# Differential attention: the norm sums of split squares as float32r products, ScalarE's weight split placed behind the copies of the probabilities, first weight tiles subtracted by GpSimd

## The chip, the cores and the metric

One NeuronCore of a Trainium2 chip runs the whole program as one launch. The metric is the device time of one execution in microseconds (us), less is better. A change is timed by the median of several executions.

Engines: PE is TensorE, ACT is ScalarE, DVE is VectorE, POOL is GpSimd, SP issues the transfers from memory.

## What is computed

The reference is two transformer blocks of two layers each, over 256 tokens (272 with 16 meta tokens in the second block) of width 1024. The change lies in one mixer of the second block, the differential attention with 8 heads:

```
q, k, v = split(h @ w_in)
q = rms_norm(q.reshape(.., 8, 2, 64), g0);  k = rms_norm(k.reshape(.., 8, 2, 64), g1)
logits = q . k * 64**-0.5 + bias            # two maps m for every head
p = softmax(where(visible, logits, -1e30))
pd = p[0] - lam * p[1]
o = pd @ v                                  # 128 values of a head
o = rms_norm(o, subln) * (1 - lambda_init)
```

Two sums of squares across partitions belong to it: one over the 64 rows of each map for q and k, one over the 128 rows of a head's output.

## The kernel before

The program is written by hand, engine by engine: each engine has one list of instructions, and semaphores say what each waits for. Nothing is reordered: a wait holds up everything behind it on its engine.

**Weights.** All products are made in three float32r products (`product`, L1592 to L1603): high part of the weights by high and low part of the moving side, then low part of the weights by the high part. Weights come in chunks into two slots in turn. For each chunk SP loads `raw` (L381), ACT copies it to `w_hi` (L703), and DVE or POOL subtracts `raw - w_hi` into `w_lo`. SP loads the next chunk of a slot when the low parts of the one before are there (`rest_ready`), ACT overwrites `w_hi` when PE has used it (`weights_used`).

**The mixer (`diff_mixer`, stage "diff").** Chunk i holds the q, k and v columns of head i, three tiles of 128x1024, and PE makes parts 0, 1 and 2 of them in round i. Beside the parts of head i each round does steps of the two heads before: sums of squares, logits and turned values of head h = i-1, turned probabilities, outputs and output sums of head b = i-2. PE's order in a round is: part 0, `sums`(h), part 1, `turn_probs`(b), half of part 2, `logits`(h), `turn_values`(h), `outputs`(b), the rest of part 2, `out_sums`(b). A last stretch behind round 7 finishes heads 6 and 7 between early products of the output projection (`early`).

- `sums` (L1800) multiplies the squares `asq` by `halves`, a 0/1 matrix, in float32: two products of 128x272. `out_sums` (L1844) multiplies `osq` by `ones`, one such product.
- ACT in round i: logarithm and exponential for the norms of h (L855, L856), `y_hi` (L849), copies of the turned probabilities of b (L861, L862), square of the outputs (L872), copies of the values (L877, L878), squares of head i (L881), exponentials of the logits of h (L886), logarithm and exponential for the output norm (L890, L891), and last the weight split of chunk i+2 (L893, the copy itself L703), 128x3072 in one instruction.
- DVE subtracts the first tile of chunks 2 to 7 (`first_tile_of`, L1140), POOL the second and third (L641, L643, the instruction itself L512). Part 0 waits for the first tile (`tile_rest`), part 1 for all three (`rest_ready`, L1753).

```
mm(to, lhsT=w_hi[slot][:, w], rhs=hi[:, k, cols], start=start and i == 0, stop=False)
mm(to, lhsT=w_hi[slot][:, w], rhs=lo[:, k, cols], start=False, stop=False)
ins = mm(to, lhsT=w_lo[slot][:, w], rhs=hi[:, k, cols], start=False, stop=stop and i == len(order) - 1)
```

## Time and profile before

| what | us |
|---|---|
| time, median of 3 runs (lowest, highest) | 1695.86 (1695.57, 1695.9) |
| time of the profiled execution | 1696.9 |
| span of the profiled execution | 1695.1 |
| PE busy | 1671.7 (99%) |
| ACT busy | 835.7 (49%) |
| DVE busy | 953.3 (56%) |
| POOL busy | 736.3 (43%) |

The span runs from the first to the last instruction of the core; the time of the same execution is 1.8 us more. The mixer takes the stretch from about 824 us to 950 us of the span. Records of matmuls overlap: a record of 0.29 us stands every 0.126 us, so what a product takes is read from the distance of the starts.

### The profile page before, as it was taken

How to read it: one execution, taken by the hardware profiler on the slowest of the kernel's cores; microseconds unless marked ns; L12 is line 12 of the kernel's file. 1: busy time of each engine (PE TensorE's matmuls, PEld its weight loads, DVE VectorE, ACT ScalarE, POOL GpSimd, SP SyncE). 2: the span in 40 equal slices, each digit the busy share in tenths (PEclk: the TensorE clock that was granted, in tenths of full speed). 3: DMA queues.
4: the chain of work that ended last, by engine and by line, in shares of the span. 5: the costliest groups of instructions: out<-in, count | busy, mean ns of one | idle time of the engine just before them, and what ended most of it. 6: DMA issues, size and time to landing. Idle time of an engine off the chain costs nothing.

```text
span 1695.1 us, 34373 instructions
## 1 busy us (share of the span) xinstructions
PE 1671.7 (99%) x13441; PEld 1630.9 (96%) x13441; DVE 953.3 (56%) x1188; ACT 835.7 (49%) x1161; POOL 736.3 (43%) x488
## 2 busy tenths in 40 slices
PE   7999999999999999999999999999999999999999
PEld 6999999999999999999999899999999988899999
DVE  6685556633655556545456755455555567665553
ACT  5445454555544544444476644444444446654442
POOL 6235553254555545553332355533554324245520
PEclk9999999999999999999999999999999999999999
DMA  7658876643787756676643466765667741357673
GB/s 205 175 163 231 232 201 187 171 113 100 214 229 195 206 155 174 173 198 174 166 120 89 121 178 173 198 174 149 173 173 195 184 106 51 100 151 196 175 213 110
DMA packets 538562, 283.55 MB, mean 167 GB/s; under 512 B 12112, under 2 KB 532817, under 8 KB 538481
## 3 DMA queue, kind: packets, MB, share of 16 engines
q1 hardware_dynamic: 538065, 281.30, 60.8%
q0 software_dynamic: 352, 1.09, 0.3%
q8 instruction: 59, 0.97, 0.2%
q14 instruction: 22, 0.18, 0.0%
q10 hardware_dynamic: 64, 0.02, 0.0%
HBM read 281.29 MB, written 5.53 MB: 169 GB/s over the span
## 4 chain that ended last, share of the span: by engine, by line
PE 87%; DVE 5%; ACT 4%; DMA 2%; POOL 1%; issue 1%; SPq 0%; POOLq 0%; ACTq 0%; DVEq 0%
PE bank L1600 26%; PE bank L1602 26%; PE bank L1601 25%; DVE w_lo L1113 2%; PE bank L1641 2%; PE bank L1985 2%; ACT w_hi L703 1%; DMA raw<-in_w_down 1%; PE bank L1948 1%; DVE xg_lo L1124 1%; DMA raw<-in_ffn_wi 1%; POOL up L588 1%; PE bank L2018 1%; PE bank L1820 0%; ACT w_hi L1032 0%
## 5 line engine op out<-in xcount | busy, mean ns | idle before, releaser
L1600 PE MATMUL bank<-xg_hi,w_hi 128*128 128x272 f32 (+1 forms) x2520 | 724.2, 287 | 0.2 <-DVE w_lo L1113 0.2
L1602 PE MATMUL bank<-xg_hi,w_lo 128*128 128x272 f32 (+1 forms) x2520 | 718.9, 285 | 0.0
L1601 PE MATMUL bank<-xg_lo,w_hi 128*128 128x272 f32 (+1 forms) x2520 | 717.1, 285 | 0.0
L1113 DVE TENSOR_TENSOR w_lo<-raw,w_hi 128x2048 fp32r<-128x2048 f32 (+3 forms) x200 | 501.2, 2506 | 263.3 <-ACT w_hi L703 263.1
L703 ACT ACTIVATE w_hi<-raw 128x2048 fp32r<-128x2048 f32 (+3 forms) x212 | 442.0, 2085 | 266.7 <-PE bank L1602 262.0
L1600 PEld LDWEIGHTS bank<-xg_hi,w_hi 128*128 128x128 f32 x2520 | 475.2, 189 | 3.0 <-issue 1.5
L1602 PEld LDWEIGHTS bank<-xg_hi,w_lo 128*128 128x128 f32 x2520 | 475.5, 189 | 0.0
L1601 PEld LDWEIGHTS bank<-xg_lo,w_hi 128*128 128x128 f32 x2520 | 474.2, 188 | 0.7
L588 POOL TENSOR_TENSOR up<-gate,up 128x256 f32<-128x256 f32 (+1 forms) x132 | 304.4, 2306 | 253.0 <-ACT gate L1039 252.9
L1600 PE MATMUL bank<-act_hi,w_hi 128*128 128x256 f32 (+1 forms) x1056 | 300.9, 285 | 0.5 <-DVE w_lo L1113 0.2
L1601 PE MATMUL bank<-act_lo,w_hi 128*128 128x256 f32 (+1 forms) x1056 | 300.7, 285 | 0.0
L1602 PE MATMUL bank<-act_hi,w_lo 128*128 128x256 f32 (+1 forms) x1056 | 300.5, 285 | 0.0
L540 POOL TENSOR_TENSOR ssq<-ssq,sq 128x256 f32<-128x256 f32 (+1 forms) x64 | 142.0, 2218 | 241.9 <-ACT sq L718 227.6
L1041 ACT ACTIVATE act_hi<-up 128x256 f32 (+3 forms) x132 | 56.1, 425 | 340.7 <-POOL up L588 340.7
L1600 PEld LDWEIGHTS bank<-act_hi,w_hi 128*128 128x128 f32 x1056 | 198.8, 188 | 1.1 <-DVE w_lo L1113 1.1
L1602 PEld LDWEIGHTS bank<-act_hi,w_lo 128*128 128x128 f32 x1056 | 198.9, 188 | 0.0
L1601 PEld LDWEIGHTS bank<-act_lo,w_hi 128*128 128x128 f32 x1056 | 198.7, 188 | 0.0
L1515 DVE TENSOR_TENSOR gate<-bank,rstd 128x256 f32<-128x256 f32 (+1 forms) x132 | 57.2, 433 | 197.0 <-PE bank L1602 193.3
L512 POOL TENSOR_TENSOR w_lo<-raw,w_hi 128x1024 fp32r<-128x1024 f32 (+3 forms) x27 | 82.1, 3041 | 154.8 <-ACT w_hi L703 128.6
L590 POOL TENSOR_TENSOR act_lo<-up,act_hi 128x256 f32 (+1 forms) x132 | 100.1, 758 | 97.4 <-ACT act_hi L1041 97.4
L1454 DVE SCALAR_TENSOR_TENSOR x<-bank,x 128x256 f32<-128x256 f32 (+3 forms) x80 | 32.9, 427 | 85.9 <-PE bank L1602 85.3
L1124 DVE SCALAR_TENSOR_TENSOR xg_lo<-x,gains,xg_hi (+2 forms) x72 | 64.1, 911 | 7.6 <-ACT xg_hi L723 5.1
(307 smaller groups left out, 1909.1 us busy)
## 6 DMA issues: line engine op xcount, KB each, us to landing
raw<-in_ffn_wi SPq DMA_DIRECT2D x176, 512.0 KB, 4.9
raw<-in_ffn_wo SPq DMA_DIRECT2D x32, 1408.0 KB, 7.1
raw<-in_w_gate SPq DMA_DIRECT2D x44, 512.0 KB, 4.0
raw<-in_w_up SPq DMA_DIRECT2D x44, 512.0 KB, 5.2
raw<-in_w_down SPq DMA_DIRECT2D x16, 1408.0 KB, 7.1
raw<-in_a_w_in SPq DMA_DIRECT2D x24, 512.0 KB, 5.3
raw<-in_a_in SPq DMA_DIRECT2D x20, 512.0 KB, 6.4
raw<-in_w_o SPq DMA_DIRECT2D x16, 512.0 KB, 4.8
```

The source lines that it names most:

```text
L512: return gp.tensor_tensor(w_lo[slot][:, t], raw[slot][:, t], w_hi[slot][:, t].bitcast(F32), ALU.subtract)
L540: gp.tensor_tensor(ssq[:, c], ssq[:, c], sq[:, s, c] if squares is None else squares, ALU.add).then_inc(ssq_ready, 1)
L588: gp.tensor_tensor(up, gate, up, ALU.mult).then_inc(act_full, 1)
L590: gp.tensor_tensor(tile(f.lo, c, f.act_cols), up, tile(f.hi, c, f.act_cols).bitcast(F32), ALU.subtract).then_inc(act_ready, 1)
L703: act.activation(w_hi[slot][:, 0:stage.size], raw[slot][:, 0:stage.size], ACT.Copy).then_inc(head_ready, 1)
L1041: act.activation(tile(f.hi, c, f.act_cols), f.up[:, s, f.act_cols], ACT.Copy).then_inc(act_hi_ready, 1)
L1113: v.tensor_tensor(w_lo[slot][:, 0:n], raw[slot][:, 0:n], w_hi[slot][:, 0:n].bitcast(F32), ALU.subtract).then_inc(rest_ready, 1)
L1124: ins = v.scalar_tensor_tensor(out=tile(lo, d, cols), in0=src, scalar=column(gains, gain + d), in1=tile(hi, d, cols).bitcast(F32), op0=ALU ...
L1515: v.tensor_tensor(f.gate[:, s, f.act_cols], bank[:, 2 * s, 0:n], rstd[:, f.cols], ALU.mult).then_inc(gate_ready, 1)
L1600: mm(to, lhsT=w_hi[slot][:, w], rhs=hi[:, k, cols], start=start and i == 0, stop=False)
L1601: mm(to, lhsT=w_hi[slot][:, w], rhs=lo[:, k, cols], start=False, stop=False)
L1602: ins = mm(to, lhsT=w_lo[slot][:, w], rhs=hi[:, k, cols], start=False, stop=stop and i == len(order) - 1)
```

## The change

The squares are split like the weights: ACT copies `asq` to `asq_hi` and `osq` to `osq_hi` (float32r), POOL subtracts the rest into `asq_lo` and `osq_lo` (`low_squares`, `low_outputs`), and PE adds two float32r products for each old float32 one. This holds for all eight heads of `sums` and for the output sums of heads 0 to 5; those of heads 6 and 7 stay as they were. `out_sums` of head b moves from the end of round b+2 to behind part 0 of round b+3. ACT's weight split of chunks 2 to 7 moves from the end of round i to behind the copies of the turned probabilities of round i+1, and becomes two instructions, the first tile with a signal of its own (`diff_head`). The first tiles of chunks 2 to 7 are subtracted by POOL, no longer by DVE. Two constant matrices are copied to float32r at the start.

```diff
--- before.py
+++ after.py
...
@@ -523,6 +527,8 @@
                                     pattern=[[-1, P]], channel_multiplier=1))
             settle(gp.memset(halves[0:HD, 0:HD], 1.0))
             settle(gp.memset(halves[HD:P, HD:P], 1.0))
+            gp.tensor_copy(halves_r[:, :], halves[:, :])
+            gp.tensor_copy(ones_r[:, :], ones[:, :])
             settle(gp.memset(vis[0:HD, META + HD:KEYS_A], NEG))
             settle(gp.memset(vis[0:HD, KEYS_A + TOK - HD:LOGB], NEG))
             gp.sem_inc(consts, 1)
@@ -635,12 +641,33 @@
             gp.wait_ge(weights_used, st["diff"].first)
             gp.memset(apt0[:, :], 0.0)
             gp.memset(avn[:, 0, :], 0.0).then_inc(a_padded, 1)
+            def low_squares(i):
+                gp.wait_ge(a_sq_hi, i + 1)
+                if i:
+                    gp.wait_ge(a_sums, i)
+                gp.tensor_tensor(asq_lo[:, :, :], asq[:, :, :], asq_hi[:, :, :].bitcast(F32), ALU.subtract).then_inc(a_sq, 1)
+            def low_outputs(b):
+                gp.wait_ge(a_osq_hi, b + 1)
+                if b:
+                    gp.wait_ge(a_osum, b)
+                gp.tensor_tensor(osq_lo[:, :], osq[:, :], osq_hi[:, :].bitcast(F32), ALU.subtract).then_inc(a_osq, 1)
+            low_squares(0)
             for c in range(2, 8):
                 g, n = st["diff"].first + c, KT * P
                 gp.wait_ge(rest_ready, g)
+                gp.wait_ge(diff_head, c - 1)
+                gp.tensor_tensor(w_lo[g % 2][:, 0:n], raw[g % 2][:, 0:n], w_hi[g % 2][:, 0:n].bitcast(F32), ALU.subtract).then_inc(tile_rest, 1)
                 split(g, n, 2 * n)
-                gp.wait_ge(tile_rest, first_tiles(st["diff"], c))
                 split(g, 2 * n, 3 * n).then_inc(rest_ready, 1)
+                if c >= 3:
+                    low_outputs(c - 3)
+                low_squares(c - 1)
+            low_outputs(5)
+            low_squares(7)
             g = st["wo2"].first + 1
             gp.wait_ge(tile_head, 5)
             gp.tensor_tensor(w_lo[g % 2][:, 0:n], raw[g % 2][:, 0:n], w_hi[g % 2][:, 0:n].bitcast(F32), ALU.subtract).then_inc(wo2_tile, 1)
@@ -860,6 +887,12 @@
                         act.wait_ge(a_turned, b + 1)
                         act.activation(apt[:, :], bank[:, 3, 0:384], ACT.Copy)
                         act.activation(apt0[0:META, :], bank[0:META, 4, 0:TOK], ACT.Copy).then_inc(a_pt, 1)
+                    if 1 <= i < 7:
+                        g, n = first + i + 1, KT * P
+                        act.wait_ge(landed[g % 2], chunks.landed[g])
+                        act.wait_ge(weights_used, g - 1)
+                        for t, signal in ((slice(0, n), diff_head), (slice(n, 3 * n), head_ready)):
+                            act.activation(w_hi[g % 2][:, t], raw[g % 2][:, t], ACT.Copy).then_inc(signal, 1)
                     if i == 8:
                         g, n = first + 9, KT * P
                         act.wait_ge(landed[g % 2], chunks.landed[g])
@@ -869,7 +902,14 @@
                             act.activation(w_hi[g % 2][:, t], raw[g % 2][:, t], ACT.Copy).then_inc(signal, 1)
                     if b >= 0:
                         act.wait_ge(a_o, b + 1)
-                        act.activation(osq[:, :], bank[:, 5, 0:TOK], ACT.Square).then_inc(a_osq, 1)
+                        if b:
+                            act.wait_ge(a_osq, b)
+                        squares = act.activation(osq[:, :], bank[:, 5, 0:TOK], ACT.Square)
+                        if b < 6:
+                            settle(squares)
+                            act.activation(osq_hi[:, :], osq[:, :], ACT.Copy).then_inc(a_osq_hi, 1)
+                        else:
+                            squares.then_inc(a_osq, 1)
                     if 0 <= h < 8:
                         act.wait_ge(a_vt, h + 1)
                         if not h:
@@ -878,7 +918,10 @@
                         act.activation(avn[:, 1:3, :], bank[:, 4, P:3 * P].rearrange("p (a b) -> p a b", b=P), ACT.Copy).then_inc(a_v, 1)
                     if i < 8:
                         act.wait_ge(parts_read, 2 * mixer_order(st["diff"], i) + 2)
-                        act.activation(asq[:, :, :], aqkv[:, i % 2, 0:2, :], ACT.Square).then_inc(a_sq, 1)
+                        if i:
+                            act.wait_ge(a_sq, i)
+                        settle(act.activation(asq[:, :, :], aqkv[:, i % 2, 0:2, :], ACT.Square))
+                        act.activation(asq_hi[:, :, :], asq[:, :, :], ACT.Copy).then_inc(a_sq_hi, 1)
                     if 0 <= h < 8:
                         act.wait_ge(a_max, h + 1)
                         for t, c in enumerate((COL_A, COL_B, COL_M)):
@@ -889,7 +932,7 @@
                         act.wait_ge(a_osum, b + 1)
                         settle(act.activation(oln[:, :], bank[:, 3, 0:TOK], ACT.Ln, bias=eps[:, 0:1], scale=1.0 / P))
                         act.activation(oln[:, :], oln[:, :], ACT.Exp, scale=-0.5).then_inc(a_orms, 1)
-                    if i < 7:
+                    if i == 6:
                         split_ahead(first + i)
                     if i == 8:
                         tile_ahead(st["wo2"])
@@ -1321,9 +1364,7 @@
                         rest_of_output(b - 1)
                     take_part(0)
                     if 0 <= h < 8:
-                        if h < 6:
-                            first_tile_of(stage.first + h + 2)
-                        elif h == 6:
+                        if h == 6:
                             v.wait_ge(rest_ready, stage.first + h + 2)
                             split_ahead(stage.first + h)
                         v.wait_ge(a_logits, h + 1)
@@ -1802,7 +1843,8 @@
                     if h:
                         pe.wait_ge(a_max, h)
                     for m in range(2):
-                        ins = mm(bank[:, 6 + m, 0:TOK], lhsT=halves[:, :], rhs=asq[:, m, :], start=True, stop=True)
+                        mm(bank[:, 6 + m, 0:TOK], lhsT=halves_r[:, :], rhs=asq_hi[:, m, :], start=True, stop=False)
+                        ins = mm(bank[:, 6 + m, 0:TOK], lhsT=halves_r[:, :], rhs=asq_lo[:, m, :], start=False, stop=True)
                     ins.then_inc(a_sums, 1)
                 def turn_values():
@@ -1843,7 +1885,11 @@
                 def out_sums():
                     pe.wait_ge(a_osq, h + 1)
-                    mm(bank[:, 3, 0:TOK], lhsT=ones[:, :], rhs=osq[:, :], start=True, stop=True).then_inc(a_osum, 1)
+                    if h >= 6:
+                        mm(bank[:, 3, 0:TOK], lhsT=ones[:, :], rhs=osq[:, :], start=True, stop=True).then_inc(a_osum, 1)
+                        return
+                    mm(bank[:, 3, 0:TOK], lhsT=ones_r[:, :], rhs=osq_hi[:, :], start=True, stop=False)
+                    mm(bank[:, 3, 0:TOK], lhsT=ones_r[:, :], rhs=osq_lo[:, :], start=False, stop=True).then_inc(a_osum, 1)
                 return sums, turn_values, logits, turn_probs, outputs, out_sums
@@ -1858,15 +1904,17 @@
                     sums, turn_values, logits, _, _, _ = steps[i - 1] if i else [None] * 6
-                    _, _, _, turn_probs, outputs, out_sums = steps[i - 2] if i > 1 else [None] * 6
-                    for step in (lambda: part(0), sums, lambda: part(1), turn_probs,
-                                 lambda: part(2, range(4)), logits, turn_values, outputs, lambda: part(2, range(4, KT)), out_sums):
+                    _, _, _, turn_probs, outputs, _ = steps[i - 2] if i > 1 else [None] * 6
+                    out_sums = steps[i - 3][5] if i > 2 else None
+                    for step in (lambda: part(0), out_sums, sums, lambda: part(1), turn_probs,
+                                 lambda: part(2, range(4)), logits, turn_values, outputs, lambda: part(2, range(4, KT))):
                         if step:
                             step()
                 sums, turn_values, logits, turn_probs, outputs, out_sums = steps[7]
                 early(2, 0, range(5))
+                steps[5][5]()
                 sums()
                 early(2, 1, range(5))
                 steps[6][3]()
```

The order of the instructions on POOL before, for chunks 2, 3 and the start of 4 (slots 0 and 1 in turn; L512 is the subtraction of one tile):

```order
L512 TENSOR_TENSOR w_lo0<-raw0,w_hi0 128x1024 [waits head_ready,rest_ready]
L512 TENSOR_TENSOR w_lo0<-raw0,w_hi0 128x1024 [waits head_ready,tile_rest]
L512 TENSOR_TENSOR w_lo1<-raw1,w_hi1 128x1024 [waits head_ready,rest_ready]
L512 TENSOR_TENSOR w_lo1<-raw1,w_hi1 128x1024 [waits head_ready,tile_rest]
L512 TENSOR_TENSOR w_lo0<-raw0,w_hi0 128x1024 [waits head_ready,rest_ready]
```

In the changed kernel POOL has these for chunks 3 and 4; L663 and L516 are the tiles of the weights, L656 the outputs' low part, L649 the squares':

```order
L663 TENSOR_TENSOR w_lo1<-raw1,w_hi1 128x1024 [waits diff_head,rest_ready]
L516 TENSOR_TENSOR w_lo1<-raw1,w_hi1 128x1024 [waits head_ready] x2
L656 TENSOR_TENSOR osq_lo<-osq,osq_hi 128x272 [waits a_osq_hi]
L649 TENSOR_TENSOR asq_lo<-asq,asq_hi 128x544 [waits a_sums,a_sq_hi]
L663 TENSOR_TENSOR w_lo0<-raw0,w_hi0 128x1024 [waits diff_head,rest_ready]
L516 TENSOR_TENSOR w_lo0<-raw0,w_hi0 128x1024 [waits head_ready] x2
L656 TENSOR_TENSOR osq_lo<-osq,osq_hi 128x272 [waits a_osum,a_osq_hi]
L649 TENSOR_TENSOR asq_lo<-asq,asq_hi 128x544 [waits a_sums,a_sq_hi]
```

Two instructions of a chunk have become five, and the low parts of the squares, for which PE waits behind part 0, stand behind the three tiles of the next chunk.

On PE, the end of part 0, the sums and the start of part 1, before:

```order
L1600 MATMUL bank<-xg_hi,w_hi 128x272
L1601 MATMUL bank<-xg_lo,w_hi 128x272
L1602 MATMUL bank<-xg_hi,w_lo 128x272
L1805 MATMUL bank<-asq,halves 128x272 [waits a_max,a_sq]
L1805 MATMUL bank<-asq,halves 128x272
L1600 MATMUL bank<-xg_hi,w_hi 128x272 [waits parts_read,rest_ready]
```

And in the changed kernel:

```order
L1642 MATMUL bank<-xg_lo,w_hi 128x272
L1643 MATMUL bank<-xg_hi,w_lo 128x272
L1891 MATMUL bank<-osq_hi,ones_r 128x272 [waits a_osq]
L1892 MATMUL bank<-osq_lo,ones_r 128x272
L1846 MATMUL bank<-asq_hi,halves_r 128x272 [waits a_max,a_sq]
L1847 MATMUL bank<-asq_lo,halves_r 128x272
L1846 MATMUL bank<-asq_hi,halves_r 128x272
L1847 MATMUL bank<-asq_lo,halves_r 128x272
L1641 MATMUL bank<-xg_hi,w_hi 128x272 [waits parts_read,rest_ready]
```

Both sums now stand in one place, the output sums ahead; `a_osq` and `a_sq` are signals of POOL's two subtractions there.

On ACT, the copies of the turned probabilities and what follows, in the changed kernel (before, L872's square followed the copies at once, and the split of 128x3072 stood behind the logarithm and exponential of `oln`):

```order
L888 ACTIVATE apt<-bank 128x384 [waits a_turned]
L889 ACTIVATE apt<-bank 16x272
L895 ACTIVATE w_hi<-raw 128x1024 [waits weights_used,landed1]
L895 ACTIVATE w_hi<-raw 128x2048
L907 ACTIVATE osq<-bank 128x272 [waits a_osq,a_o]
L910 ACTIVATE osq_hi<-osq 128x272 [waits a_step]
L917 ACTIVATE avn<-bank 16x128 [waits a_vt]
```

The weight copy now waits, through its place, for the turned probabilities.

## Rows read from the trace of the kernel before

**Rows 1.** Windows: us, busy of PE, PEld, DVE, ACT, POOL, granted clock, DMA.

```profile
872.60:886.30 13.70, 13.70 (x107) 12.91 (x105) 8.46 (x20) 9.53 (x26) 4.76 (x2) 1.00 0.44 116
```

**Rows 2.** Waits of PE from 827 to 950 us: total, times, longest.

```profile
PE bank L1820 <- DVE aqkv L1317: 0.6, 1, 0.6
PE bank L1641 <- DVE apd L1347: 0.5, 1, 0.5
```

**Rows 3.** Timeline of PE: start, us, line, tile, count.

```profile
836.65 1.08 PE L1805 MATMUL bank<-asq,halves 128*128 128x272 f32 x4
...
879.56 0.92 PE L1641 MATMUL bank<-ident,apd 128*128 128x128 f32 x6
...
885.91 0.62 PE L1846 MATMUL bank<-osq,ones 128*128 128x272 f32 x2
...
886.49 0.28 PE L1601 MATMUL bank<-xg_lo,w_hi 128*128 128x272 f32 x1
...
889.39 1.08 PE L1805 MATMUL bank<-asq,halves 128*128 128x272 f32 x4
...
890.43 0.29 PE L1601 MATMUL bank<-xg_lo,w_hi 128*128 128x272 f32 x1
...
916.91 1.08 PE L1805 MATMUL bank<-asq,halves 128*128 128x272 f32 x4
```

**Rows 4.** Timeline of ACT in one round, idle before in brackets.

```profile
875.75 2.76 ACT L703 ACTIVATE w_hi<-raw 128x3072 fp32r<-128x3072 f32 x1
878.41 0.66 ACT L855 ACTIVATE bank<-bank,eps 128x544 f32<-128x544 f32 x1
879.10 0.61 ACT L856 ACTIVATE bank<-bank 128x544 f32<-128x544 f32 x1
...
880.51 0.49 ACT L861 ACTIVATE apt<-bank 128x384 f32<-128x384 f32 x1 [0.47 <-PE bank L1641]
880.90 0.37 ACT L862 ACTIVATE apt<-bank 16x272 f32<-16x272 f32 x1
884.60 0.40 ACT L872 ACTIVATE osq<-bank 128x272 f32<-128x272 f32 x1 [3.32 <-PE bank L1842]
```

**Rows 5.** Timeline of POOL in the same round, and two rows of the last mixer.

```profile
878.64 2.39 POOL L512 TENSOR_TENSOR w_lo<-raw,w_hi 128x1024 fp32r<-128x1024 f32 x1 [7.15 <-ACT w_hi L703]
882.89 2.37 POOL L512 TENSOR_TENSOR w_lo<-raw,w_hi 128x1024 fp32r<-128x1024 f32 x1 [1.86 <-DVE w_lo L1140]
...
1420.39 1.29 POOL L659 TENSOR_TENSOR qs<-qs 128x512 f32<-128x512 f32 x1 [5.22 <-ACT qs L966]
1421.64 2.13 POOL L668 TENSOR_TENSOR bias<-bias,score 128x288 f32<-128x288 f32 x2
```

**Rows 6.** Groups by line and form: count, busy us, mean ns.

```profile
L588 POOL TENSOR_TENSOR up<-gate,up 128x272 f32<-128x272 f32 x66 | 153.6, 2328 | 136.1 <-ACT gate L1039 136.1
L590 POOL TENSOR_TENSOR act_lo<-up,act_hi 128x272 f32 x66 | 51.2, 776 | 49.2 <-ACT act_hi L1041 49.2
L512 POOL TENSOR_TENSOR w_lo<-raw,w_hi 128x1024 fp32r<-128x1024 f32 x18 | 42.8, 2379 | 75.2 <-ACT w_hi L703 60.8 <-DVE w_lo L1140 11.0 <-ACT w_hi L800 3.4
L869 ACT ACTIVATE w_hi<-raw 128x1024 fp32r<-128x1024 f32 x2 | 2.0, 1039 | 0.0
```

**Rows 7.** Source line L881: min, median, max ns, first and last start.

```profile
L881 ACT ACTIVATE asq<-aqkv x8: 657/657/658, 832.4 to 927.0; 128x544 f32<-128x544 f32 x8
```

**Rows 8.** Timeline: one subtraction of DVE beside POOL and alone.

```profile
864.88 2.38 POOL L512 TENSOR_TENSOR w_lo<-raw,w_hi 128x1024 fp32r<-128x1024 f32 x1 [7.10 <-ACT w_hi L703]
...
866.80 0.76 DVE L1305 TENSOR_TENSOR y_lo<-oy,y_hi 128x272 fp32r<-128x272 f32 x1
...
921.00 0.43 DVE L1305 TENSOR_TENSOR y_lo<-oy,y_hi 128x272 fp32r<-128x272 f32 x1
```

**Rows 9.** Groups of DVE by form, 800 to 950 us: scaling and combining the probabilities.

```profile
L1344 DVE TENSOR_SCALAR apd<-al,ars 128x272 f32<-128x272 f32 x8 | 2.8, 356 | 0.0
L1347 DVE SCALAR_TENSOR_TENSOR apd<-al,ars,apd 128x272 f32<-128x272 f32 x8 | 4.0, 496 | 0.0
```

More of the change, by code:

```diff
@@ L127, in two_blocks @@
         ident, ones, halves, tri = (sb(n, [P, P]) for n in ("ident", "ones", "halves", "tri"))
+        halves_r, ones_r = sb("halves_r", [P, P], F32R), sb("ones_r", [P, P], F32R)
         eps, gains, small = sb("eps", [P, 1]), sb("gains", [P, P + KT]), sb("small", [P, 4])
@@ L162, in two_blocks @@
             aqkv = sb("aqkv", [P, 2, 3, TOK], F32, ph)
+            asq_hi, asq_lo = (sb(n, [P, 2, TOK], F32R, ph) for n in ("asq_hi", "asq_lo"))
+            osq_hi, osq_lo = (sb(n, [P, TOK], F32R, ph) for n in ("osq_hi", "osq_lo"))
             asq, avn = sb("asq", [P, 2, TOK], F32, ph), sb("avn", [P, 3, P], F32, ph)
```

1 line of the change is left out of this document (added).

## The prediction

> **What bounds the kernel now.** I read the windows first. In one round of the mixer [rows 1] PE is busy in all of 13.70 us at full granted clock, while POOL works 4.76 us of it, ACT 9.53 and DVE 8.46. The waits of PE [rows 2] say the same over the whole mixer: 1.1 us in two places, both behind the last round. So PE's own work sets the time here, and every microsecond that goes from PE counts, as long as nothing else becomes slower than a round. The round's length comes from the starts of the `sums` in the timeline of PE [rows 3]: two rounds lie between 889.39 and 916.91, 13.76 us each. The timelines of ACT and POOL [rows 4, 5] show who has room. ACT makes the weight copy of 2.76 us as the last thing of a round, which holds up the logarithm behind it, and stands idle for 3.32 us between the copies of the probabilities and the squares of the outputs. POOL waits 7.15 us for the copy, does a tile, waits 1.86 us for DVE's tile, and does another.
>
> **What PE saves.** The two float32 products of `sums` start at 889.39; the second product behind them starts at 890.43, and a float32r product stands every 0.126 us (24 of part 0 fit between 886.36 and 889.39, where 886.36 is 886.49 less 0.126). So they take 890.43 - 0.13 - 889.39 = 0.91 us. The output sum takes 886.36 - 885.91 = 0.45 us [rows 3]. Four float32r products take 0.50 and two take 0.25. That is 0.41 us for each of 8 heads and 0.20 for each of 6: **4.5 us** in all. PE's own round becomes 13.15 us.
>
> **What POOL gets.** Before, two tiles of 2.38 us [rows 5, 6]. Now three, the low part of the outputs and the low part of the squares. A subtraction of the first one's size took 0.78 (128x272) and a tile of 1024 columns 2.38, both in rows 6; along this line 544 columns take 1.36. A round of POOL is 7.14 + 0.78 + 1.36 = 9.3 us, which fits in 13.15. But its place decides, not its sum. By the order of the instructions, the low squares that `sums`(h) waits for stand on POOL behind all three tiles of the next chunk, and those wait for a weight copy that stands on ACT behind the turned probabilities, which PE makes behind part 1, behind the `sums` before. That closes a loop from one `sums` to the next:
>
> - `sums` 0.50, part 1 3.03 (24 products);
> - turned probabilities, to ACT's first copy: 880.51 - 879.56 = 0.95 [rows 3, 4];
> - both copies, to the weight copy: 0.39 (880.90 - 880.51), and 0.27 (0.37 less the 0.10 by which ACT's records overlap);
> - weight copy of the first tile 1.04 [rows 6], to POOL 0.13 (878.51 to 878.64) [rows 4, 5];
> - three tiles 7.14, low outputs 0.78, low squares 1.36, less 0.16 for four overlaps of POOL's records (1421.64 begins 0.04 before the end of the one of 1420.39) [rows 5];
> - to PE 0.03.
>
> The sum is **15.46 us**, against 13.76 before: 1.70 us more. PE's work in it is 13.15, so PE stands for 2.3 us in each such round, first for the low outputs (`out_sums` is ahead of `sums` on PE), then for the low squares; everything behind it on PE is queued, part 1 first. The saving of PE is swallowed whole in these rounds. The loop turns five times (chunks 3 to 7, between `sums`(1) and `sums`(6)): **+8.5 us**.
>
> **Before the loop.** `sums`(0) keeps its place at 836.65: the squares start at 832.4 [rows 7], the high copy (a copy of the same shape; I take the square's 0.66) ends by 833.8, the low part by 835.3. Chunk 2 waits for no probabilities: from 836.65 the sums' records end 0.67 later, logarithm and exponential take 0.66 and 0.61 with gaps of 0.03 [rows 4], weight copy 1.04, three tiles and low squares 8.5, hand-overs 0.16, overlaps -0.2: PE can start `sums`(1) at about 848.3. It started at 916.91 - 5 x 13.76 = 848.1. **+0.2 us**.
>
> **Behind the loop.** PE saves 0.41 for each of `sums`(6) and (7) and 0.20 for the output sum of head 5. Against that `sums`(7) waits for the square, its copy (0.66) and POOL (1.36); PE arrives after 15 early products (1.9 us), and I lay this out to a wait of 0.5. The exponentials of head 6 stand on ACT behind two more copies (0.40 as the square of L872, and 0.66), and this stretch is where PE already waited for DVE [rows 2]: between 0 and 1.1 us, I take 0.8, for PE arrives earlier too. **+0.3 us**, bounds -1.0 and +0.8.
>
> **What costs nothing.** ACT has 1.06 us more to copy in each round and hides it in the idle 3.32 us and in PE's new waits. The weight copy in two pieces begins 5.4 us later than before (881.17 against 875.75), and the raw slot is free later by about as much, with a whole round of cover before ACT wants the next load. If that cover went, the copy's start would slip and with it the loop, one for one. DVE loses six tiles, which nobody waits for. The two copies at the start of the program are short and POOL idles there.
>
> **The sum.** 0.2 + 8.5 + 0.3 = +9.0 us. The sum is made on the profiled execution, whose time is 1696.9 (span 1695.1); the median of the runs is 1695.86, 1.0 less, and I take the difference to be the same there: **1704.9 us**.
>
> **Unknown prices.** POOL's subtraction of 544 columns is not in the mixer's trace: not below 0.78, the price of half of it; above, there is a row where 272 columns take 2.33 us (L588) [rows 6], in the feed-forwards, beside DVE's long subtractions of weights. I take 1.36, since two of POOL's forms lie on one line and DVE has no long subtraction left in these rounds. Each 0.1 us is 0.5 us of time.
>
> **Where DVE and POOL meet.** DVE's `y_lo` takes 0.43 alone and 0.76 when POOL's tile runs: it starts at 866.80, the tile ends at 867.26, and 867.26 + 0.3 is its end [rows 8]. So they exclude each other. In the new round the three instructions that combine the probabilities on DVE (0.50 at the most [rows 9]) come due while POOL is at the low squares. By my layout POOL is there first, and DVE waits up to 1 us, covered by part 1. Were DVE first, POOL would wait 0.5 in each of five rounds. The sum counts nothing for it.
>
> The Trainium skill, "GPSIMD Engine Reference", section "Key points", says that the two share their SBUF interfaces, and that VectorE's instructions in a 2-port performance mode contend as well as those with two inputs in SBUF. The second half agrees with `y_lo`; for the first half no row here has POOL beside such an instruction.
>
> **Rivals.**
>
> *DVE delays POOL.* The scaling of the probabilities has one input, takes 0.36 where the combining takes 0.50 for the same size [rows 9], and starts about half a microsecond after the exponentials, just when POOL goes from the low outputs to the low squares. If it excludes POOL too, POOL waits 0.36 in each of five rounds: +1.8, 1706.7. With one combining instead, +2.5: 1707.4. All six in a row would be up to 2.6 a round and 1718, which needs POOL to lose each time. The page's rule named above would make the scaling one of these. Chance 0.26.
>
> *The gain lands.* If POOL's chain fitted in PE's round, the time would be 1695.86 - 4.5 + 0.9 for the stretch behind: 1692.3, faster. The place is POOL's five instructions of 9.1 us; it decides at 15.46 - 13.15 = 2.3 us less, or 0.46 off each of the five. For it: the sum of POOL's work is far from a round. Against: 18 tiles have a mean of 2.379 and nothing of the chain overlaps. Chance 0.04.
>
> *It cancels.* A loop of 13.8 us, 1.7 less than mine, gives about 1696.4. That would need POOL's small subtractions and the hand-overs to be almost free. Chance 0.03.
>
> *POOL's subtractions are slow.* At 2.33 for each of the two (the L588 row), the loop is 2.5 us longer: +12.6, 1717.5. Against: DVE has no long instruction there. Chance 0.04.
>
> **Numbers.** My forecast has the rest, 0.63. Its own bounds are the loop within 0.3 us a round (five times) and the stretch behind: 1702.4 to 1707.2. To leave out no more than 2 in 10 with the first rival in, and allowing for collisions of more than one instruction, the range is 1702.0 to 1710.0. A measurement of this kernel can tell some 0.2% from no change, 3.4 us. Faster: 0.04. Same: 0.03. Slower: 0.93.
>
> **What would show it.** The distance of the `sums` on PE is about 15.4 us between the second and the seventh. PE waits for POOL's low outputs for about 1.2 us and then for the low squares for about 1.1 us, five times each. POOL runs its five instructions of a chunk without a gap and idles some 6.3 us before the first, for ACT's weight copy. The four products of `sums` take 0.50. ACT's copy follows the probabilities without idle time. The forecast is wrong if the distance is 13.2 to 13.8, if PE waits for part 1's weights instead, or if the low squares take other than 1.3 to 1.6 us.

## The result and the profile after

The changed kernel takes **1710.8 us** (median of 4 runs, 1710.24 to 1713.82) against 1695.88 for the kernel before (4 runs beside them, 1695.57 to 1696.38): ratio 1.009, 95% interval 1.0078 to 1.0102. It is slower, as forecast, but by 14.9 us and not by 9.0, and 0.8 us above the top of the range. The profiled execution took 1710.96 us with a span of 1709.2, 14.1 more than that of before.

The whole loss lies in the mixer. The first update of `x` behind it, on DVE, stands at 950.14 before and at 964.48 after:

```profile
950.14 0.79 DVE L1454 SCALAR_TENSOR_TENSOR x<-bank,x 128x272 f32<-128x272 f32 x2 [1.17 <-PE bank L1602]
```

```profile
964.48 0.79 DVE L1495 SCALAR_TENSOR_TENSOR x<-bank,x 128x272 f32<-128x272 f32 x2 [1.17 <-PE bank L1643]
```

Both kernels start the first `sums` at 836.65, so the mixer's stretch from there became 127.83 us instead of 113.49: 14.34 more. The timeline of PE after the change, at the first product of each head's `sums` (start, us, line, tile, and in brackets the idle time before it), shows where:

```profile
836.65 0.29 PE L1846 MATMUL bank<-asq_hi,halves_r 128*128 128x272 f32 x1
...
848.41 0.39 PE L1846 MATMUL bank<-asq_hi,halves_r 128*128 128x272 f32 x1 [0.56 <-POOL asq_lo L649]
...
863.98 0.40 PE L1846 MATMUL bank<-asq_hi,halves_r 128*128 128x272 f32 x1 [0.79 <-POOL asq_lo L649]
...
879.57 0.40 PE L1846 MATMUL bank<-asq_hi,halves_r 128*128 128x272 f32 x1 [0.78 <-POOL asq_lo L649]
...
893.86 0.39 PE L1891 MATMUL bank<-osq_hi,ones_r 128*128 128x272 f32 x1 [1.12 <-POOL osq_lo L656]
...
895.15 0.39 PE L1846 MATMUL bank<-asq_hi,halves_r 128*128 128x272 f32 x1 [0.77 <-POOL asq_lo L649]
...
912.22 0.39 PE L1846 MATMUL bank<-asq_hi,halves_r 128*128 128x272 f32 x1 [0.78 <-POOL asq_lo L649]
...
929.32 0.40 PE L1846 MATMUL bank<-asq_hi,halves_r 128*128 128x272 f32 x1 [0.79 <-POOL asq_lo L649]
```

The starts of the heads' `sums` are 15.57, 15.59 and 15.58 us apart, then 17.07 and 17.10; before, 13.76 each [rows 3]. The waits of PE from 824 to 970 us (total, times, longest) have two new entries in place of next to nothing [rows 2]:

```profile
PE bank L1891 <- POOL osq_lo L656: 5.6, 5, 1.1
PE bank L1846 <- POOL asq_lo L649: 4.8, 7, 0.8
```

POOL and ACT in the round before 895.15 are the forecast loop: the copies of the probabilities, the weight copy straight behind them, then five instructions of POOL without a gap. ACT first:

```profile
884.15 0.49 ACT L888 ACTIVATE apt<-bank 128x384 f32<-128x384 f32 x1 [1.94 <-PE bank L1682]
884.54 0.37 ACT L889 ACTIVATE apt<-bank 16x272 f32<-16x272 f32 x1
884.82 2.84 ACT L895 ACTIVATE w_hi<-raw 128x1024 fp32r<-128x1024 f32 x2
```

and POOL, whose idle time before the first tile is the 6.48 in brackets:

```profile
886.00 2.38 POOL L663 TENSOR_TENSOR w_lo<-raw,w_hi 128x1024 fp32r<-128x1024 f32 x1 [6.48 <-ACT w_hi L895]
888.33 4.76 POOL L516 TENSOR_TENSOR w_lo<-raw,w_hi 128x1024 fp32r<-128x1024 f32 x2
893.04 0.76 POOL L656 TENSOR_TENSOR osq_lo<-osq,osq_hi 128x272 fp32r<-128x272 f32 x1
893.76 1.33 POOL L649 TENSOR_TENSOR asq_lo<-asq,asq_hi 128x544 fp32r<-128x544 f32 x1
```

What I had not foreseen stands in the windows by round (us, busy of PE, PEld, DVE, ACT and POOL with counts, granted clock, DMA share, GB/s). Up to 895 us the clock is 1.00, as in [rows 1]. Then it is 0.90, 0.89 and 0.89:

```profile
863.90:879.50 15.60, 13.68 (x105) 12.65 (x105) 8.25 (x20) 11.01 (x28) 9.11 (x6) 1.00 0.40 105
879.50:895.00 15.50, 13.69 (x105) 12.65 (x105) 8.15 (x20) 10.92 (x28) 9.02 (x6) 1.00 0.38 98
895.00:912.00 17.00, 15.18 (x105) 14.16 (x105) 8.14 (x20) 10.93 (x27) 9.01 (x6) 0.90 0.36 94
912.00:928.00 16.00, 14.69 (x103) 13.88 (x103) 7.15 (x19) 10.51 (x26) 7.99 (x6) 0.89 0.21 59
928.00:943.00 15.00, 14.20 (x98) 13.30 (x98) 9.81 (x18) 8.43 (x19) 2.93 (x3) 0.89 0.50 140
...
896.00:900.00 4.00, 4.00 (x22) 4.00 (x21) 2.92 (x9) 1.67 (x3) 0.00 (x0) 0.57 1.12 279
```

The last row shows for the first of these rounds that it is one piece of some 3.4 us at the lower level of 1.2 GHz. It begins half a microsecond after the sums, in part 1 of the round. In the timeline of PE the products stand 0.126 us apart ahead of it and 0.227 in it:

```profile
896.12 0.29 PE L1641 MATMUL bank<-xg_hi,w_hi 128*128 128x272 f32 x1
896.25 0.39 PE L1642 MATMUL bank<-xg_lo,w_hi 128*128 128x272 f32 x1
896.44 0.43 PE L1643 MATMUL bank<-xg_hi,w_lo 128*128 128x272 f32 x1
896.66 0.43 PE L1641 MATMUL bank<-xg_hi,w_hi 128*128 128x272 f32 x1
...
899.61 0.33 PE L1642 MATMUL bank<-xg_lo,w_hi 128*128 128x272 f32 x1
```

15 products took 899.61 - 896.25 = 3.36 us and would have taken 1.89: **1.5 us** a time, three times. So the 14.34 us are: 0.32 up to `sums`(1) (848.41 against 848.09), five rounds at 15.58 - 13.77 = 1.81, 9.05 in all, three stretches at the low clock, 4.5 (two of them in these rounds, the third behind `sums`(6)), and 0.4 more behind `sums`(6).

### The profile page after: what moved, and what is told of

Its sections match the earlier page's. It is cut to its first block, busy times and chain, and to the rows that moved or that the text cites. A ratio compares the mean times of both kernels' runs of the same rounds, so it can differ in the third digit from the quotient of the medians.

```text
span 1709.2 us, 34429 instructions
## 1 busy us (share of the span) xinstructions
PE 1673.7 (98%) x13441; PEld 1633.0 (96%) x13441; DVE 950.9 (56%) x1182; ACT 844.6 (49%) x1181; POOL 765.7 (45%) x510
## 4 chain that ended last, share of the span: by engine, by line
PE 84%; DVE 5%; ACT 4%; POOL 3%; DMA 2%; issue 1%; SPq 0%; POOLq 0%; ACTq 0%; DVEq 0%
PE bank L1641 25%; PE bank L1643 25%; PE bank L1642 25%; DVE w_lo L1156 2%; PE bank L2033 2%; PE bank L1682 2%; ACT w_hi L730 1%; POOL w_lo L516 1%; DMA raw<-in_ffn_wi 1%; DVE xg_lo L1167 1%; POOL up L594 1%; POOL w_lo L663 1%; PE bank L2066 1%; ACT w_hi L1075 0%; DMA xin<-in_x 0%
## 5 line engine op out<-in xcount | busy, mean ns | idle before, releaser
L730 ACT ACTIVATE w_hi<-raw 128x2048 fp32r<-128x2048 f32 (+3 forms) x206 | 425.5, 2065 | 266.8 <-PE bank L1643 261.2
L516 POOL TENSOR_TENSOR w_lo<-raw,w_hi 128x1024 fp32r<-128x1024 f32 (+3 forms) x27 | 82.0, 3049 | 96.3 <-ACT w_hi L730 81.0
```

Of the source, the lines that this page charges most:

```text
L516: return gp.tensor_tensor(w_lo[slot][:, t], raw[slot][:, t], w_hi[slot][:, t].bitcast(F32), ALU.subtract)
L730: act.activation(w_hi[slot][:, 0:stage.size], raw[slot][:, 0:stage.size], ACT.Copy).then_inc(head_ready, 1)
```

## The experiments

Each edit is made on the changed kernel. "Mixer" is the stretch from the first `sums` to the first update of `x` behind it: 113.49 us before, 127.83 after. It is read from one profiled execution of each kernel. The medians take in the rest of the program too, where low stretches of the clock come and go: the window from 0 to 20 us has 0.83 before and after, 0.91 with the waits filled and 1.00 with DVE's tile.

### The idle time of PE filled with dummy products

```diff
+                    def fill(n, start):
+                        if i >= start:
+                            pe.wait_ge(a_max, i - 1)
+                            for _ in range(n):
+                                mm(bank[:, 6, 0:TOK], lhsT=ones_r[:, :], rhs=xg_hi[:, 0, :], start=True, stop=True)
-                    for step in (lambda: part(0), out_sums, sums, ...
+                    for step in (lambda: part(0), lambda: fill(8, 3), out_sums, lambda: fill(6, 3), sums, ...
```

> The change with PE kept at work where it waits: in rounds 3 to 7 PE makes 8 products of 128x272 into a bank that nobody reads before the output sums, and 6 before the norm sums (about 1.0 and 0.75 us, no more than the two waits). Idle theory: the clock dips of the changed kernel come from PE standing idle for 1.1 and 0.8 us in every round. Then the distance of the norm sums is 15.6 us in all rounds, the granted clock is 1.00 throughout the mixer, and the time is 1710.8 - 4.6 = 1706.2. Rival, the dips have another cause than PE's idle time: the distances of 17.1 us and the granted clock of 0.89 to 0.90 stay, 1710.8.

Measured: 1705.43 us (before: 1696.85), ratio 1.0052, interval 1.0035 to 1.0069: 5.4 us below the change, of which the mixer has 4.3 (123.50 us). The `sums` stand 15.6 us apart in every round (893.85, 909.46, 925.08), and the windows that had the low clock now read

```profile
895.00:911.00 16.00, 15.82 (x124) 14.79 (x124) 8.65 (x22) 11.37 (x29) 9.12 (x5) 1.00 0.41 108
911.00:927.00 16.00, 15.82 (x124) 14.80 (x124) 8.64 (x21) 12.02 (x28) 9.13 (x5) 1.00 0.25 70
```

The 14 dummy products a round stand where PE waited for POOL anyhow, and the low clock is gone. The clock's share is shown, and it comes from PE's waits: the rest of the kernel is the same. What is left is +8.6 us by the medians and +10.0 in the mixer, around the forecast of +9.0. The two differ because the profiled execution of this kernel reaches the mixer 1.43 us earlier than that of before (835.22 against 836.65), with a shorter low stretch at its start.

### The products in float32 again, the rest of the change kept

The high copies on ACT and the low parts on POOL go; the three tiles on POOL, the two-piece weight copy behind the probabilities and the later place of the output sum stay.

```diff
-                        mm(bank[:, 6 + m, 0:TOK], lhsT=halves_r[:, :], rhs=asq_hi[:, m, :], start=True, stop=False)
-                        ins = mm(bank[:, 6 + m, 0:TOK], lhsT=halves_r[:, :], rhs=asq_lo[:, m, :], start=False, stop=True)
+                        ins = mm(bank[:, 6 + m, 0:TOK], lhsT=halves[:, :], rhs=asq[:, m, :], start=True, stop=True)
```

> The change with the products of the squares in float32 again (no high copies on ACT, no low parts on POOL); the moved weight copy, the third tile on POOL and the moved output sums stay. Queue theory: what costs is that PE waits for the low parts behind three tiles. Then PE waits for nothing on POOL, the distance of the norm sums is PE's 13.76 us and the time 1696.0, within 1 of before. Rival, the weights themselves come too late (three tiles on POOL behind the late copy): PE waits before part 1 in each round, 1698 or more.

Measured: 1696.65 us, ratio 1.0002, interval 0.9992 to 1.0012. PE waits for POOL nowhere, and the `sums` in its timeline start at 861.60, 875.36 and 889.13, 13.76 and 13.77 apart.

The mixer takes 113.97 us, 0.5 more than before. So the moved tiles and the moved copy cost next to nothing by themselves. They cost when the low parts that PE needs are queued behind them.

### ScalarE's weight copy ahead of the wait for the turned probabilities

```diff
-                    if b >= 0:
-                        act.wait_ge(a_turned, b + 1)
...
                     if 1 <= i < 7:
                         g, n = first + i + 1, KT * P
...
+                    if b >= 0:
+                        act.wait_ge(a_turned, b + 1)
```

> The change with ACT's weight copy moved ahead of the wait for the turned probabilities (it stands right behind the exponential of the norms). Queue theory: the loop loses part 1, the turned probabilities and their copies, so that POOL's chain fits in a round; PE waits at most 0.5 us for the low squares in a round, distance 13.2 to 13.7 us, no clock dips, time about 1695.6 (within 1.5). Rival, DVE and POOL shut each other out so often that the chain stays longer than 14.5 us: 1702 or more.

Measured: 1696.97 us, ratio 1.0004, interval 0.9995 to 1.0014; mixer 113.9. The distances are 13.26 to 14.00 us, up to 0.3 more than expected, and the longest wait 0.8, not 0.5. One block of ACT moved by one place turns +14.9 us into +0.1: the turned probabilities no longer close the loop. The waits of PE for POOL shrink from 10.4 us to

```profile
PE bank L1846 <- POOL asq_lo L649: 2.0, 4, 0.8
```

### The low parts between POOL's second and third tile

```diff
                 split(g, n, 2 * n)
-                split(g, 2 * n, 3 * n).then_inc(rest_ready, 1)
                 if c >= 3:
                     low_outputs(c - 3)
                 low_squares(c - 1)
+                split(g, 2 * n, 3 * n).then_inc(rest_ready, 1)
```

> The change with POOL's low outputs and low squares placed between the second and the third tile of a chunk. The sums then don't wait; part 1 waits for the third tile instead. Queue theory: the loop loses the hand-over to the sums and 0.5 us of sums, distance about 15.0 us, one wait of about 1.8 us before part 1 in place of two of 1.1 and 0.8; 1695.9 + 8 = 1704 without clock dips. Idle theory of the clock: PE idles as much in a round as in the change, in one piece, so dips come too, up to +4.6: 1704 to 1708.6. If low parts behind the tiles were not what PE waits for, the distance would stay 15.6.

Measured: 1705.67 us, ratio 1.0053, interval 1.0036 to 1.007; distance 15.08 (896.00, 911.07, 926.15), one stretch at the low clock. It lies in the first round of the loop (16.60 us, from 849.24), and the five waits of the same length behind it bring none. The wait changes its name and stays:

```profile
PE bank L1641 <- POOL w_lo L516: 9.3, 6, 1.6
```

The same 9.1 us of POOL end in the round, and what comes last is now the third tile. Another order of POOL's own five instructions doesn't open the loop.

### The first tile back on DVE

```diff
-                gp.wait_ge(diff_head, c - 1)
-                gp.tensor_tensor(w_lo[g % 2][:, 0:n], ...).then_inc(tile_rest, 1)
...
+                            v.wait_ge(diff_head, h + 1)
+                            v.tensor_tensor(w_lo[g % 2][:, t], ...).then_inc(tile_rest, 1)
```

> The change with the first tile of chunks 2 to 7 subtracted by DVE again (as soon as its high part is there), POOL keeps the second and third. Queue theory: the loop loses a tile of 2.33 us but now begins with the second piece of ACT's copy (1.9 us, less 0.1), because POOL has nothing to do before it: distance about 15.0 us, PE waits about 1.1 and 0.7, time 1702.0 without clock dips. If it was the number of tiles on POOL alone that mattered, the distance would be 13.2 and the time 1693. Idle theory of the clock: idle time is only 0.5 us a round less than in the change, so one to three dips of 1.5 us: 1703.5 to 1706.5.

Measured: 1703.79 us, ratio 1.0044, interval 1.0028 to 1.0059; distance 15.03, clock 1.00 in the whole mixer, mixer 120.6. POOL has 6.75 us to do in 16 and PE still waits for it:

```profile
PE bank L1849 <- POOL asq_lo L649: 4.8, 7, 0.8
PE bank L1894 <- POOL osq_lo L656: 2.9, 5, 0.6
```

A tile less on POOL gives 0.55 us a round, not 2.38, since the two that are left wait for the second piece of ACT's copy, 1.8 us behind the first (POOL idles 8.28 us, not 6.48). The share of busy time misleads here: the place of the work decides.

### Dummy products only ahead of the output sum

> The change with PE kept at work for about 1.0 us before the output sums in rounds 3 to 7, but left idle for 0.8 us before the norm sums. The distance by the queue stays 15.6. Idle theory: the less PE stands idle, the fewer dips; with 0.8 us in one piece a round fewer than three: 1706 to 1708. Rival, the dips come from the wait before the norm sums alone, or from a change of work between waits: still three, 1710.8.

Measured: 1706.99 us (1706.62 to 1709.23), ratio 1.0061, interval 1.0045 to 1.0076. PE is idle for 0.8 us five times, right ahead of the norm sums, which the waits show without a releaser:

```profile
PE bank L1846 <- issue: 4.1, 5, 0.8
```

and the granted clock is 1.00 in each window from 848 to 928 us. So the second wait, alone and of this length, brought no low clock in this trace. The mixer takes 123.43 us, the same as with both waits filled, so the 1.6 us by which the median is above that kernel's lie outside it. One low stretch there is at 1500 to 1520 us (0.91), in another mixer; the filled kernel has one too, at 1400 to 1420, so this alone does not explain them.

### More work at the end of POOL's round

An extra subtraction of the squares' size, the same one twice, ahead of the low outputs.

```diff
+                gp.wait_ge(a_sq_hi, c)
+                gp.wait_ge(a_sums, c - 1)
+                settle(gp.tensor_tensor(asq_lo[:, :, :], asq[:, :, :], asq_hi[:, :, :].bitcast(F32), ALU.subtract))
                 if c >= 3:
                     low_outputs(c - 3)
```

> The change with POOL's low squares done twice for chunks 2 to 7, the extra one ahead of the low outputs (1.33 us and about 0.1 to settle). Queue theory: the loop is that much longer, distance 17.0 us, +1.4 in each of six rounds, 1710.8 + 8.5 = 1719.3 with three clock dips as in the change. Idle theory of the clock: with 3.3 us idle a round there are more dips, up to one in every round, each 1.5 us: 1719 to 1724. Rival, POOL's queue isn't what sets the rounds: less than +4.

Measured: 1725.05 us (1723.55 to 1725.62), ratio 1.0165, interval 1.0149 to 1.018. The first round of the loop has 16.99 us (849.53 to 866.52), the slope of one subtraction as expected. The next has 19.53, since from here on the clock is low in every round:

```profile
863.60:879.00 15.40, 13.12 (x81) 12.20 (x82) 9.00 (x18) 7.29 (x14) 6.29 (x5) 0.78 0.40 103
879.00:895.00 16.00, 12.71 (x90) 11.80 (x89) 7.22 (x15) 9.06 (x24) 7.99 (x6) 0.89 0.37 99
```

The time is 1 us above the range that I expected. Low stretches cost more than the 1.5 us that I had put in for each: against the 16.99 us of the first round, the four next have 2.54, 1.45, 2.34 and 1.34 more, and in windows of 1 us the stretches last some 6.8 and 3.4 us in turn. Over the traces so far more idle time of PE in a round goes with more low stretches in the mixer: none in the filled kernels (0 and 0.8 us idle) and with DVE's tile (1.35), one with the low parts in the middle (1.6), three in the change (1.9), and here (3.0 to 3.3) one at each of the five pairs of waits. These are counts in one execution each, and no threshold is read from them.

### A first attempt at a version below both

Early copy, DVE's tile, and head 7's squares in float32, together.

> What the queue theory says should beat both: the split squares, with ACT's weight copy right behind the exponential of the norms (as in the early copy run), the first tile on DVE, and the squares of head 7 in float32 as before. POOL's chain fits in PE's round: no wait of PE from the second round on over 0.3 us, distance 13.2 to 13.4 us, no dips, 1.7 us below before: 1694.3. If the early copy holds up the copies of the probabilities by more than the 0.2 us that I lay out, or DVE and POOL shut each other out, it comes out at before's time or above.

Measured: 1696.07 us (11 runs), ratio 0.9996, interval 0.9987 to 1.0005. The distance is 13.5, but it is no faster than before by anything that was measured: 1.1 us went to four waits of PE for the copies of the probabilities, now behind the weight copy on ACT, and about 1.5 to one low stretch, behind the last round (0.90 and 0.89 from 927 to 943 us), where PE waits for DVE first.

### The copy back at the end of the round

```diff
-                    if 1 <= i < 7:
-                        g, n = first + i + 1, KT * P
...
+                    elif i < 6:
+                        g, n = first + i + 2, KT * P
                         for t, signal in ((slice(0, n), diff_head), (slice(n, 3 * n), head_ready)):
```

> The change with ScalarE's weight copy (still in its two pieces) put back to the end of a round, behind the logarithm and exponential of the output norm, as before; products, low parts and the three tiles on POOL stay. Loop theory (the chain sums, part 1, turned probabilities, weight copy, three tiles, low parts binds): the copy no longer waits for the turned probabilities, POOL starts its tiles several us earlier in each round, POOL's work of 9.1 us fits in a round, and the distance of the sums falls from 15.58 to PE's own 13.2 to 13.4. PE waits for POOL at most 0.2 us a round, the clock stays at 1.00 in rounds 3 to 7. Time: before minus 2.0 us (five rounds at about -0.4 us) plus 1.0 (head 7's squares and the stretch behind) = 1694.9 against a before of 1695.9, range 1693.5 to 1697. Rival (the amount of work given to POOL, not its place, makes the loss): distance stays at 15 or more, time above 1702. Second rival (PE waits of 0.5 us or more remain at the low squares, as with the early copy): distance 13.6 and 1696 to 1697.

Measured: 1707.21 us (before: 1697.72), ratio 1.006, interval 1.0047 to 1.0074. **A clear miss**, and by neither of the rivals: the time is that of the first one (above 1702), but its distance of 15 or more is not there. PE hardly waits for POOL any more, it waits for the turned probabilities:

```profile
PE bank L1682 <- DVE apd L1388: 10.6, 7, 5.6
PE bank L1846 <- POOL asq_lo L649: 1.8, 2, 1.2
```

DVE's timeline has the reason, in the first such round and in a later one. Three combinings, which took 0.93 us before and after, take 7.11 and 3.08:

```profile
848.33 0.71 DVE L1385 TENSOR_SCALAR apd<-al,ars 128x144 f32<-128x144 f32 x3
849.07 7.11 DVE L1388 SCALAR_TENSOR_TENSOR apd<-al,ars,apd 128x144 f32<-128x144 f32 x3
...
868.56 0.71 DVE L1385 TENSOR_SCALAR apd<-al,ars 128x144 f32<-128x144 f32 x3
869.31 3.08 DVE L1388 SCALAR_TENSOR_TENSOR apd<-al,ars,apd 128x144 f32<-128x144 f32 x3
```

and POOL's timeline shows what ran meanwhile:

```profile
848.90 2.39 POOL L663 TENSOR_TENSOR w_lo<-raw,w_hi 128x1024 fp32r<-128x1024 f32 x1 [2.06 <-ACT w_hi L936]
851.24 4.91 POOL L516 TENSOR_TENSOR w_lo<-raw,w_hi 128x1024 fp32r<-128x1024 f32 x2
...
869.97 2.38 POOL L663 TENSOR_TENSOR w_lo<-raw,w_hi 128x1024 fp32r<-128x1024 f32 x1 [2.88 <-ACT w_hi L936]
872.31 4.91 POOL L516 TENSOR_TENSOR w_lo<-raw,w_hi 128x1024 fp32r<-128x1024 f32 x2
```

The combinings end when POOL's tile ends (872.35 and 872.39), in the first round when all three do (856.15 and 856.18). In narrower windows of that round each of the three combinings stands for one tile of POOL: they start at 849.07, 851.38 and 853.88 and take 2.39, 2.57 and 2.30 us. It is the meeting that [rows 8] show for `y_lo`, but `y_lo` is wanted late and the probabilities at once. The two-piece copy had let POOL begin 1.8 us before the whole copy was made, just in the way. The first gap is 20.83 us (846.89 to 867.72), with 5.55 idle and a granted clock of 0.79 in the window behind it; the four after it are 14.4. Together, 7.06 + 4 x 0.64 = 9.6 us. What this adds to the change: its move of the copy behind the probabilities keeps POOL's tiles clear of the combinings, and pays for it with the loop.

### The same with head 7's squares in float32

> The kernel of the run before, with the squares of head 7 alone summed in float32 again (no high copy on ACT, no low part on POOL, two float32 products). Theory: sums(7) no longer waits for ACT's copy and POOL's subtraction (0.66 + 1.33 us, of which about 1.2 is seen by PE), and pays 0.41 for the float32 products: about 0.7 us less than that kernel, 1694.2 against a before of 1695.9 (range 1693 to 1696.5). This is the candidate to beat both kernels. Rival (the stretch behind the last round is set by DVE, not by sums(7)): the same time as the run before within 0.3 us.

Measured: 1706.87 us, ratio 1.006, interval 1.0046 to 1.0074. The forecast of 1694.2 stood on that of the kernel above and missed with it. It is 0.34 less than the kernel above, within the scatter of both. PE waits for POOL 0.6 us instead of 1.8, but for the probabilities 11.0 instead of 10.6.

### POOL starting behind the whole copy

The last kernel but one with the two pieces in the other order. Nothing else differs.

```diff
-                        for t, signal in ((slice(0, n), diff_head), (slice(n, 3 * n), head_ready)):
+                        for t, signal in ((slice(n, 3 * n), head_ready), (slice(0, n), diff_head)):
```

> The kernel of e9 (copy at the end of a round) with the two pieces of ScalarE's copy in the other order: the large one first, the first tile's last. The work is the same; only POOL's first tile may begin some 1.8 us later, when the whole copy is made. What e9 showed: POOL's tile began at 869.97, in the middle of DVE's three combinings of probabilities (869.31), which then took 3.08 us instead of 0.93 (7.11 in the first such round), and PE stood for the turned probabilities. Port theory (DVE's instruction with two inputs in SBUF waits for POOL's): the combinings end at about 870.3 before POOL begins at 871.7, take 0.93 us in all, the wait of PE for the turned probabilities goes to 0.1 us or less, the gap of 20.8 us between the second and third sums shrinks to about 13.4, and the distance becomes 13.2 to 13.5. Time: before minus 2.5 plus 1.5 = before minus 1.0, 1695 to 1696.5 against a before of 1696.4 (range -2.5 to +1.5 us of before). Rival (the copy's length on ACT, not POOL's tile, delays the combinings): nothing changes, distance 14.4 and before plus 9.5. Second rival (y_lo on DVE now meets a whole tile of POOL and holds up the logits behind it): distance 13.7 to 14.0, before plus 1 to 3.

Measured: 1695.81 us (before: 1696.30), ratio 0.9997, interval 0.9988 to 1.0006: 11.4 us less than with the first tile's piece ahead, 10.0 when each is held against the kernel before timed beside it, and 11.6 less in the mixer (112.95 against 124.56). The combinings are whole again in DVE's timeline,

```profile
875.51 0.93 DVE L1388 SCALAR_TENSOR_TENSOR apd<-al,ars,apd 128x144 f32<-128x144 f32 x3
```

and POOL begins 1.5 us behind their end:

```profile
877.98 2.39 POOL L663 TENSOR_TENSOR w_lo<-raw,w_hi 128x1024 fp32r<-128x1024 f32 x1 [4.08 <-ACT w_hi L936]
```

The copy's length is out as a cause, since it didn't change. The distance of the `sums` on PE is 13.40, 0.25 above the 13.15 worked out for PE alone:

```profile
860.54 0.29 PE L1846 MATMUL bank<-asq_hi,halves_r 128*128 128x272 f32 x1
...
873.95 0.39 PE L1846 MATMUL bank<-asq_hi,halves_r 128*128 128x272 f32 x1
...
887.35 0.39 PE L1846 MATMUL bank<-asq_hi,halves_r 128*128 128x272 f32 x1
```

### The same with head 7's squares in float32

> The kernel of e11 with the squares of head 7 alone summed in float32 (as in e10). Theory: head 7's sums no longer wait for the copy and POOL's subtraction, 0.3 to 0.7 us less than e11 (e10 was 0.34 below e9, within the noise of both). This is the last candidate for a version below both kernels: before minus 1.5 us, range before -3 to +1. If e11 shows the second rival instead, this is as far below e11.

Measured: 1695.00 us (11 runs, before 1696.30 with 21), ratio 0.9993, interval 0.9984 to 1.0002. The mixer is 112.25 us against 113.49, so the profile shows a gain of 1.2 us, and the medians 1.3. The interval takes in no change, so this version is not shown faster than the kernel before, and it is the best of those tried.

## Why the prediction was right, and where it was wrong

**What PE saves.** Right: the four float32r products of `sums` without a wait stand at their 0.126 us (836.65 and behind). The gain is there for the taking only when nothing binds, and it is smaller than forecast: with the loop open, the round is 13.40 us (the last kernels), not 13.15, so a round saves 0.36 us and not 0.61.

**The loop.** Right in kind and in size: 15.46 forecast, 15.58 measured. The waits were forecast as 1.2 us for the low outputs and 1.1 for the low squares and are 1.12 and 0.78. The idle time of POOL is 6.48 us (6.3 forecast), the low squares take 1.33 us (1.36 forecast, within 1.3 to 1.6). Two edits that open it, by the early copy and by the products in float32, give back the loss, and the extra subtraction of 1.33 us made the first round 1.4 longer (16.99 against 15.58). Of the 0.12 us by which the loop is longer than forecast, the `sums` have 0.11: they were put in at 0.50, but behind the wait the second product starts 0.23 us after the first and part 1 begins at 880.18, 0.61 after 879.57.

**Before and behind the loop.** 0.2 forecast and 0.32 measured; 0.3 and 0.4. The terms listed for the stretch before the loop add up to 848.15, not to the 848.3 that the prediction took, so its closeness there is in part luck.

**The sum.** This is the step that failed: "0.2 + 8.5 + 0.3 = +9.0 us". It has no term for the granted clock. I had given PE 2.3 us of standing in every round and then costed the work behind each wait at the full clock of [rows 1], which is a row of a PE that never stood. The trace has three low stretches that cost 1.5 us each, 4.5 in all. With it the forecast would have been 1709.4. Filling the waits with dummy products took 5.4 us off, 4.3 of them in the mixer. What was left was 8.6 us above before by the medians, within 0.4 of my sum, but 10.0 in the mixer, which is the cleaner measure. The rest of the 14.34 is 0.12 us more in each of five rounds and 0.2 at both ends together. A term for the clock could have been had from the trace of the kernel before, where another mixer shows a window of PE with waits and less than the full clock:

```profile
1380.00:1400.00 20.00, 18.03 (x111) 11.95 (x109) 15.37 (x37) 10.93 (x19) 2.41 (x1) 0.91 0.27 79
```

**The range.** Its top of 1710.0 had been reached by adding collisions of DVE and POOL, which did not happen at POOL's cost. It came near the result for a reason that was not the true one, which is luck. The forecast's own bounds, 1702.4 to 1707.2, were missed by 3.6 us.

**Where DVE and POOL meet.** "Were DVE first, POOL would wait 0.5": POOL was first in all rounds, as in my layout, and its 1.33 us for the low squares show no wait. DVE waits instead, not in the combining but already in the scalings ahead of it, in the timeline of the change:

```profile
878.29 1.74 DVE L1385 TENSOR_SCALAR apd<-al,ars 128x144 f32<-128x144 f32 x3
880.07 0.93 DVE L1388 SCALAR_TENSOR_TENSOR apd<-al,ars,apd 128x144 f32<-128x144 f32 x3
```

The three scalings take 0.71 us when POOL is idle and 1.74 here: 1.03 more, ending at 880.03, after POOL's end at 879.52. Part 1 on PE covers it. So the rival "DVE delays POOL" had the right meeting and the wrong side, and cost nothing. The Trainium skill, "GPSIMD Engine Reference", section "Key points", counts VectorE's instructions in a 2-port performance mode among those that contend for the shared interfaces. The scaling, with one input, is held up beside POOL in this trace, which agrees with that; no row shows the mode it ran in.

**What I left out.** The prediction costs the move of the copy only by what it delays. It did not ask what stood at the copy's old place on the other engines. The miss with the copy at the end shows that a POOL tile there costs 7.06 us once, the low clock behind the stall included, and 0.64 in each later round.

**Open.** Why two pairs of waits (ahead of 863.98 and 879.57) are followed by a round at full clock, and the next three by a low stretch, isn't settled: the waits ahead of the norm sums differ by 0.02 us at most, those ahead of the output sums by 0.03. With the low parts in the middle it was the other way round, the first wait brought the low stretch and the later ones none. That the waits are needed is shown; what else goes into the moment is not.

## What to carry to other kernels

When a change moves a small result behind long work on a side engine's queue, follow the result around: from the waiting engine through each in-order queue back to itself. If the path closes, its length is the round, however idle the engines on it look. Where the sum then has the matrix engine standing in every round, add a bound for its clock, from the rows of any stretch with low granted clock. And before an instruction of GpSimd is started earlier, look at what VectorE does with SBUF operands in that stretch, and who waits for it: two signals in another order were worth 10 to 11 us here.

## What was not expected of the hardware

- A granted clock of half speed for some 3.4 us came in the change behind three of five pairs of PE's waits of 1.1 and 0.8 us in a round of 15.6, and cost 1.5 us each time. With waits of 2.5 and 0.5 to 0.8 us (the extra subtraction) it came at all five pairs and lasted up to 6.8 us, with 0.6 and 0.8 us (DVE's tile) it came at none.
- While POOL subtracted three tiles in a row, three short combinings of DVE stood for one tile each, 6.2 us in all (7.11 against 0.93), although each needs 0.3 us alone. The other way POOL lost little: its two tiles took 4.91 beside DVE's work and 4.76 without.
- DVE's scaling with one input in SBUF is held up by POOL as well (1.74 against 0.71 us).
